# Where GpSimd issues the v gathers: behind the u gathers of two ticks later, instead of one

## The chip, the cores and the metric

The kernel runs on one core of a Trainium2 chip, in float32. The metric is device time in microseconds (us) of one execution, median of the runs shown.

## The reference

Two small networks run one after the other on 256 tokens of width 1024. The first is two layers of attention and MLP. The second is two layers of attention (a sparse one, "nsa", then one with forget gates, "fox"), each followed by a PEER feed-forward. This feed-forward is what the change touches: every token chooses 128 experts (8 heads x 16) out of 16384 by ranking scores, and each expert is one row of a table u and one of a table v.

```python
def one_chunk(args):
    xc, ec, gc = args                  # 128 tokens, their 128 experts, their gates
    h = jax.nn.gelu(jnp.einsum('ted,td->te', u[ec], xc))
    return jnp.einsum('te,ted->td', gc.astype(h.dtype) * h, v[ec])
```

## The kernel before

The first network, and the projections of the second's first attention, come first and take about 900 us of the span. Then follow four windows: two layers times two tiles of 128 tokens. A window is 128 expert slots, and a slot is one expert for each of the 128 tokens: a gather of 128 rows of 4 KB from u and one from v, by an indirect DMA that GpSimd issues. Four slots (SLICE) are a tick, so that a window has 32 ticks (TICKS) and the whole has 128, numbered here from 0 to 127.

In each tick every engine does its part of the four slots:

- GpSimd issues the gathers (`gather`, line 2290 for u and v alike). The buffers are rings of 8 slots, two ticks (RING), one for u (`urow`) and one for v (`vrow`). A gather into a ring waits until the slot of 8 before was used: for u the semaphore `u_used`, which VectorE raises at each dot, for v the semaphore `v_used`, which TensorE raises at each slot. A u gather also waits for `routed`, the choice of its experts.
- VectorE makes the dots with the token (`expert_dots`, line 1945; 'CUSTOM_DVE_ANT_0' in the trace, with the reading of the accumulator behind it).
- ScalarE makes the gelu and the gates and writes a diagonal matrix for each slot (`expert_gates`, lines 1389, 1394 and 1400).
- TensorE multiplies this diagonal with the v rows and adds up in two banks (`expert_slice`, line 925). A slot is 4 matmul records, the slice of a tick 16.

Beside this part each of TensorE, ScalarE and VectorE runs the rest of the second network in pieces between ticks: behind the slice, gates or dots of tick k comes what the plans (`STAGES`, `nsa_plan`, `fox_plan`, `LATE_ROUTE`) put at tick k. In the plans of attention VectorE's pieces stand one tick behind TensorE's (`added_late`). Examples are the masked scores (`soften`, line 1996, from TensorE's line 1014 or 1122), the weighted values (TensorE's line 1000, VectorE's reciprocals in lines 2011 and 2179), the transposes of line 991, the projections of line 945 with weight panels that SyncE loads, and the ranking of the next window's experts (lines 1861 to 1926). At the end of each window VectorE folds the sum into the residual (`fold`, line 1954); it waits for all of the window's slices, and TensorE's next slice waits for it. Every engine's instructions stand in program order on its queue.

Of the kernel before, what the change touches and what calls it, by code (L numbers as in the profile page):

```python
# [67 lines left out]
TICKS = SLOTS // SLICE  # L68
WINDOWS = [(layer, t) for layer in range(2) for t in range(TILES)]
# [91 lines left out]
    return base + WEIGHTS[name[0]] + int(name[1])  # L161


LATE_RANKS = [24, 25, 26, 27, 35, 36, 37, 38]
CHOSEN = [[(0, 1), (1, 3), (3, P_HEADS)]] + [[(0, P_HEADS // 2), (P_HEADS // 2, P_HEADS)]] * 3
CHOICES = {"route00": [-1, 1, 7], "route01": [28, 40], "route10": [28, 40], "route11": [28, 40]}
# [2 lines left out]
def ranked_at(stage, begin, head):  # L169
    if stage == "route00":  # L170
        return [-1, -1, 0, 2, 3, 4, 5, 6][head]
    return begin + LATE_RANKS[head]

# [9 lines left out]
def piece_of(window, slot):  # L183
    return pieces_before(window) + sum(first * TOPK <= slot for first, _ in CHOSEN[window])
# [102 lines left out]
def over(base, dims):  # L287

    return bass.AP(base.tensor, base.offset, [list(base.ap[0])] + [list(d) for d in dims])


def build(nc, x, panels, gains, consts, line_consts, rel_bias, lam, subln, small, fbias, keys, u0, v0, u1, v1, out,
# [3 lines left out]
    with ExitStack() as ctx:  # L296
# [241 lines left out]
        def apart(eng, *waits):  # L538


            for s, value in waits:
                eng.wait_ge(s, value)
            eng.sem_inc(waits_passed, 1)
# [42 lines left out]
        def filled(eng, key):  # L586

            eng.wait_ge(bank_filled, NUMBER[key] + 1)
# [8 lines left out]
        @block.sync  # L597
        def _(sp):
            sp.dma_start(h[:, :, :], x.rearrange("(t p) d -> p t d", p=P)).then_inc(first_loaded, 16)

            sp.wait_ge(first_loaded, 16 * 5)
            def load(n, half, slot):
                at = slice(half * PANEL // 2, (half + 1) * PANEL // 2)
                sp.dma_start(ring[:, slot, at], panels[n, :, at]).then_inc(landed[slot][half], 16)

            for s in range(2):
                if s == 1:
                    sp.wait_ge(landed[0][1], 16)
                for half in range(2):
                    load(s, half, s)  # L610
            pairs = N_PANELS // 2
            with sp.Fori(1, pairs) as i:
                for s in range(2):
                    for half in range(2):

                        sp.wait_ge(panel_used, i * 4 + (2 * s - 3 + half))
                        load(i * 2 + s, half, s)
            for n in range(2 * pairs, N_PANELS):
                for half in range(2):
                    sp.wait_ge(panel_used, 2 * n - 3 + half)  # L620
                    load(n, half, n % 2)
            for i, key in enumerate(USES):
                n = N_PANELS + i
                if i < 2:
                    sp.wait_ge(panel_used, 2 * (n - 1))
                else:
                    filled(sp, LAST_USE.get(USES[i - 2], USES[i - 2]))
                sp.dma_start(ring[:, n % 2, :], panels[panel_source(key)]).then_inc(landed[n % 2][0], 16)
            for t in range(TILES):
                sp.wait_ge(final_ready, t + 1)  # L630
                sp.dma_start(out[t * P:(t + 1) * P, :], xn[:, t, :]).then_inc(out_landed, 16)
            sp.wait_ge(out_landed, 16 * TILES)
# [582 lines left out]
        def _(act):  # L1215
# [248 lines left out]
            def soft_exps(stage, i):  # L1464
                key = stage, in_batch("S", 0, i)[-1]
                t, _, depth = block_of(key)
                keys_of = (t + 1) * P
                if i >= 2:
                    emptied(act, (stage, f"O{i - 2}"))
                act.wait_ge(peak_ready, softened(key))  # L1470
                for j in range(BATCH):
                    a = soft_of(key)[:, j * keys_of:(j + 1) * keys_of]
                    last = f(a, a, ACT.Exp, bias=peaks[i % 2][:, j:j + 1], accum_out=totals[i % 2][:, j:j + 1])
                last.then_inc(soft_ready, 1)
# [791 lines left out]
        @block.gpsimd  # L2266
        def _(pool):
            phase = Phases(pool)
            g = nc.gpsimd

            def stage_pairs(call):

                base, kind = PAIRS * call, KIND[call]
                with pool.Fori(0, PAIRS // 2) as i:
                    for u in range(2):
                        p = i * 2 + (base + u)

                        apart(pool, (s_done, p + (AHEAD - 1)))
                        g.tensor_copy(stage[u][:, :, 0, :], pj[:, :, bass.ds(i * (2 * P) + u * P, P)])  # L2279
                        last = g.tensor_copy(stage[u][:, :, 1, :], pj[:, :, bass.ds(i * (2 * P) + (D + u * P), P)])  # L2280
                        last.then_inc(staged, 1)

            def gather(rows, tables, there, tick):

                layer, t = WINDOWS[tick // TICKS]
                for n in range(tick * SLICE, (tick + 1) * SLICE):
                    s, slot = n % RING, n % SLOTS
                    if n >= RING:
                        pool.wait_ge(u_used if rows is urow else v_used, n - RING + 1)
                    g.indirect_dma_start(out=rows[s], out_offset=None, in_=tables[layer],  # L2290
                                         in_offset=bass.IndirectOffsetOnAxis(ap=experts[:, t, slot:slot + 1], axis=0))\
                        .then_inc(there[s], 16)

            for (step, arg), meets in zip(SCHEDULE, MEETS):
                if step == "attend":
                    stage_pairs(arg)
                elif step == "dense" and arg == "in0":

                    for slot in range(2):
                        pool.wait_ge(landed[slot][1], 16)  # L2300

                    pool.wait_ge(lines_ready, 1)
                    pool.dma_start(line_dram, lines).then_inc(lines_out, 16)
                    pool.wait_ge(lines_out, 16)
                    pool.dma_start(lines_dram.rearrange("p h l -> p (h l)"),
                                   bass.AP(line_dram.tensor, 0, [[0, P], [1, HEADS * LINE]])).then_inc(lines_out, 16)

                    pool.wait_ge(lines_out, 32)
                    later = bass.AP(lines_dram.tensor, P - 1, [[HEADS * LINE - 1, P], [LINE, HEADS], [1, SEQ]])
                    early = bass.AP(lines_dram.tensor, 2 * P - 1, [[HEADS * LINE - 1, P], [LINE, HEADS], [1, P]])  # L2310
                    pool.dma_start(bias[:, :, P:S_COLS], later).then_inc(lines_in, 16)
                    pool.dma_start(bias[:, :, 0:P], early).then_inc(lines_in, 16)
                    pool.dma_start(smallw[:, :], small).then_inc(loaded, 16)
                    for dst, src, n in ((subln_row, subln, 2 * HD), (fb_row, fbias, HEADS)):
                        pool.dma_start(dst[:, :], bass.AP(src.tensor, 0, [[0, P], [1, n]])).then_inc(loaded, 16)
                    pool.wait_ge(lines_in, 32)
                    pool.wait_ge(loaded, 16 * 3)
                if meets:
                    phase()
            for n in range(8):  # L2320
                piece, t = (0, 1, 2, 4)[n // 2], n % 2
                pool.wait_ge(roped, {0: 5 + t, 1: 6, 2: 7 + t, 3: 9 + t}[n // 2])
                if n == 7:
                    filled(pool, ("middle", "T3"))
                g.tensor_copy(twin[n].rearrange("p g (a b) -> p g a b", a=2),  # L2325
                              over(pj[:, t, KV_AT + piece * GROUPS * HD:], [[HD, GROUPS], [0, 2], [1, HD]]))\
                    .then_inc(twinned, 1)
            pool.wait_ge(proj_read, 2 * AHEAD + 2 * sum(WIDTH.values()))
            g.tensor_copy(kept_v, over(pj[:, 1, KV_AT + 3 * GROUPS * HD:], [[2 * GROUPS * HD, 2], [1, GROUPS * HD]]))\
                .then_inc(v_kept, 1)  # L2330
            for tick in range(-1, len(WINDOWS) * TICKS):

                after = tick + 1
                if after < len(WINDOWS) * TICKS:
                    pool.wait_ge(routed, piece_of(after // TICKS, after % TICKS * SLICE))
                    gather(urow, (u0, u1), u_landed, after)
                if tick >= 0:
                    gather(vrow, (v0, v1), v_landed, tick)
# [71 lines left out]
```

## Time and profile before

| | |
|---|---|
| median of 3 runs | 2504.35 us (2501.98 to 2504.45) |
| the profiled execution | 2505.09 us, span 2502.9 us |
| TensorE / VectorE / ScalarE / GpSimd busy | 85% / 57% / 35% / 40% |
| DMA, mean over the span | 302 GB/s |
| mean granted TensorE clock | 0.936 |

A row of the page or of a list of groups gives a source line, the engine (PE is TensorE, PEld its weight load, DVE VectorE, ACT ScalarE, POOL GpSimd), what is written and read, a count, then the busy time and the mean of one, and behind the last bar the idle time of the engine just ahead of these instructions with what ended it. Z is the large region in which `urow`, `vrow` and `diag` lie. A row of a timeline begins with the start in us from the span's start and the duration. A row of a stretch gives the engines in the order PE, PEld, DVE, ACT, POOL.

### The profile page before, as it was taken

How to read it: one execution, taken by the hardware profiler on the slowest of the kernel's cores; microseconds unless marked ns; L12 is line 12 of the kernel's file. 1: busy time of each engine (PE TensorE's matmuls, PEld its weight loads, DVE VectorE, ACT ScalarE, POOL GpSimd, SP SyncE). 2: the span in 40 equal slices, each digit the busy share in tenths (PEclk: the TensorE clock that was granted, in tenths of full speed). 3: DMA queues.
4: the chain of work that ended last, by engine and by line, in shares of the span. 5: the costliest groups of instructions: out<-in, count | busy, mean ns of one | idle time of the engine just before them, and what ended most of it. 6: DMA issues, size and time to landing. Idle time of an engine off the chain costs nothing.

```text
span 2502.9 us, 24203 instructions
## 1 busy us (share of the span) xinstructions
PE 2139.3 (85%) x7260; PEld 1252.2 (50%) x7260; DVE 1416.0 (57%) x3004; ACT 881.8 (35%) x2125; POOL 1000.2 (40%) x1076
## 2 busy tenths in 40 slices
PE   7889999799999876789987898897899898667676
PEld 5668878678877542354433343343445343223232
DVE  3474463554465458665485744476745457584443
ACT  3445444644534322463232243222234223221121
POOL 0100000000000046556656556656656656667664
PEclk9899999899999798899999998998999999888888
DMA  8325545055545279789999999999999999999997
GB/s 312 141 75 180 199 168 194 25 177 193 176 143 210 101 317 364 288 320 386 413 412 407 401 409 357 414 412 409 386 415 359 394 412 386 366 339 377 359 380 283
DMA packets 172681, 754.69 MB, mean 302 GB/s; under 512 B 19184, under 2 KB 19344, under 8 KB 152736
## 3 DMA queue, kind: packets, MB, share of 16 engines
q0 software_dynamic: 148640, 544.05, 56.2%
q1 hardware_dynamic: 21584, 197.14, 21.2%
q10 hardware_dynamic: 2352, 12.24, 1.3%
q8 instruction: 49, 0.80, 0.1%
q14 instruction: 56, 0.46, 0.0%
HBM read 752.28 MB, written 4.22 MB: 302 GB/s over the span
## 4 chain that ended last, share of the span: by engine, by line
PE 58%; DVE 10%; issue 9%; DMA 8%; POOL 8%; ACT 3%; another core or an unknown queue 2%; DVEq 1%; ACTq 0%; POOLq 0%; SPq 0%
PE ps L925 19%; PE ps L945 9%; POOL Z L2290 8%; PE ps L670 7%; PE ps L672 7%; PE ps L671 7%; DMA Z<-v,experts 6%; DVE Z L1945 3%; DMA ring<-panels 1%; PE ps L1000 1%; PE ps L1065 1%; DVE ring_lo L1767 1%; DMA Z<-u,experts 1%; PE ps L991 1%
## 5 line engine op out<-in xcount | busy, mean ns | idle before, releaser
L925 PE MATMUL ps<-Z 128*128 128x512 f32 x2048 | 991.0, 640 | 240.8 <-DMA Z<-v,experts 123.2
L925 PEld LDWEIGHTS ps<-Z 128*128 128x128 f32 x2048 | 410.9, 206 | 782.8 <-issue 608.5
L1945 DVE CUSTOM_DVE_ANT_0 Z<-Z,ps 128x1024 f32<-128x1024 f32 x512 | 605.7, 1219 | 270.3 <-DMA Z<-u,experts 209.2
L2290 POOL DMA_INDIRECT Z<-u,experts x512 | 487.2, 951 | 378.0 <-issue 156.8
L2290 POOL DMA_INDIRECT Z<-v,experts x512 | 489.2, 955 | 350.4 <-PE ps L925 162.6
L1767 DVE TENSOR_TENSOR ring_lo<-ring,ring_hi 128x1024 fp32r<-128x1024 f32 x212 | 247.7, 1221 | 191.6 <-ACT ring_hi L1231 191.4
L945 PE MATMUL ps<-ring,o 128*128 128x512 f32 x560 | 252.3, 605 | 10.5 <-issue 9.8
L670 PE MATMUL ps<-ring_hi,xT_lo 128*128 128x512 f32 x592 | 235.6, 398 | 12.7 <-DVE xT_lo L1815 7.5
L671 PE MATMUL ps<-ring_lo,xT 128*128 128x512 f32 x592 | 231.3, 391 | 0.0
L672 PE MATMUL ps<-ring_hi,xT 128*128 128x512 f32 x592 | 231.2, 391 | 0.0
L1231 ACT CAST ring_hi<-ring 128x1024 fp32r<-128x1024 f32 x212 | 209.0, 1051 | 40.0 <-DMA ring<-panels 37.5
L1400 ACT ACTIVATE Z<-cst,wslot 128x128 f32<-128x128 f32 x512 | 165.9, 392 | 95.9 <-remote 47.9
L1389 ACT ACTIVATE hdot<-hdot 128x4 f32<-128x4 f32 x128 | 26.5, 207 | 456.8 <-issue 235.8
L945 PEld LDWEIGHTS ps<-ring,o 128*128 128x128 f32 x560 | 107.0, 194 | 142.0 <-issue 141.0
L2279 POOL COPY Z<-pj 128x256 f32 x16 | 6.5, 406 | 410.4 <-ACTq L535 361.0
L670 PEld LDWEIGHTS ps<-ring_hi,xT_lo 128*128 128x128 f32 x592 | 111.6, 189 | 43.7 <-DVE ring_lo L1767 8.7
L2325 POOL COPY ksc<-pj 128x512 f32<-128x512 f32 x5 | 3.5, 713 | 303.8 <-DVE pj L1855 297.8
L672 PEld LDWEIGHTS ps<-ring_hi,xT 128*128 128x128 f32 x592 | 111.6, 188 | 23.7
L671 PEld LDWEIGHTS ps<-ring_lo,xT 128*128 128x128 f32 x592 | 111.7, 189 | 22.5 <-issue 0.5
L1394 ACT ACTIVATE wslot<-hdot,gate_w 128x1 f32<-128x1 f32 x512 | 109.4, 285 | 9.3 <-issue 0.7
L670 PE MATMUL ps<-ring_hi,hT 128*128 128x512 f32 x256 | 100.5, 392 | 1.4 <-DVE hT L1775 1.2
L672 PE MATMUL ps<-ring_hi,hT 128*128 128x512 f32 x256 | 99.7, 389 | 0.0
(271 smaller groups left out, 1968.4 us busy)
## 6 DMA issues: line engine op xcount, KB each, us to landing
ring<-panels SPq DMA_DIRECT2D x106, 1024.0 KB, 5.0
ring<-panels SPq DMA_DIRECT2D x40, 2048.0 KB
Z<-u,experts POOLq DMA_INDIRECT x512
Z<-v,experts POOLq DMA_INDIRECT x512
gain<-gains ACTq DMA_DIRECT2D x4, 1024.0 KB, 4.8
pj<-keys ACTq DMA_DIRECT2D x4, 1024.0 KB
bias_lines<-bias_line POOLq DMA_DIRECT2D x1, 3072.0 KB, 14.9
gain<-gains ACTq DMA_DIRECT2D x5, 512.0 KB, 3.7
```

The costliest lines, as they stand in the source:

```text
L670: mm(out, b, c, start=start, stop=False)
L671: mm(out, a, d, start=False, stop=False)
L672: return mm(out, a, c, start=False, stop=stop)
L925: last = mm(ps[:, c, :], diag[s], vrow[s][:, c * NC:(c + 1) * NC], start=slot == 0, stop=slot == SLOTS - 1)
L945: last = mm(to, tokT[:, k, :], w[:, k * NC:(k + 1) * NC], start=k == 0, stop=k == KT - 1)
L1231: copy(ring_hi[:, slot, c * CH:(c + 1) * CH], ring[:, slot, c * CH:(c + 1) * CH]).then_inc(hi_ready, 1)
L1389: f(cols, cols, ACT.Gelu_apprx_tanh)
L1394: f(own[:, s:s + 1], cols[:, s:s + 1], ACT.Copy, scale=gate_w[:, t, slot + s:slot + s + 1])
L1400: f(diag[n % RING], ident, ACT.Copy, scale=own[:, s:s + 1]).then_inc(diag_ready, 1)
L1767: v.tensor_tensor(ring_lo[:, slot, at], ring[:, slot, at], ring_hi[:, slot, at].bitcast(F32), ALU.subtract).then_inc(lo_ready, 1)
L1945: v.tensor_tensor_reduce(out=row, in0=row, in1=dotted, scale=1.0, scalar=0.0, op0=ALU.mult, op1=ALU.add, accum_out=hdot[:, t, slot:slot + 1])\
L2290: g.indirect_dma_start(out=rows[s], out_offset=None, in_=tables[layer], in_offset=bass.IndirectOffsetOnAxis(ap=experts[:, t, slot:slot + 1 ...
```

## The change

The loop in which GpSimd issues the gathers starts two ticks ahead instead of one. In its turn for a tick it issues the u gathers of two ticks later, and then the v gathers of the tick itself. Nothing else changes: the same 1024 gathers with the same waits on the same rings.

```diff
+V_BEHIND = 2
...
-            for tick in range(-1, len(WINDOWS) * TICKS):
-
-                after = tick + 1
+            for tick in range(-V_BEHIND, len(WINDOWS) * TICKS):
+
+                after = tick + V_BEHIND
                 if after < len(WINDOWS) * TICKS:
                     pool.wait_ge(routed, piece_of(after // TICKS, after % TICKS * SLICE))
                     gather(urow, (u0, u1), u_landed, after)
                 if tick >= 0:
                     gather(vrow, (v0, v1), v_landed, tick)
```

On GpSimd's queue, where the expert phase begins, stand before (with the semaphores that a row waits for; the first waits of a ring's first two ticks are absent):

```order
L2290 DMA Z<-u,experts 128x1024 [waits routed]
L2290 DMA Z<-u,experts 128x1024 x3
L2290 DMA Z<-u,experts 128x1024 [waits routed]
L2290 DMA Z<-u,experts 128x1024 x3
L2290 DMA Z<-v,experts 128x1024 x4
L2290 DMA Z<-u,experts 128x1024 [waits u_used,routed]
L2290 DMA Z<-u,experts 128x1024 [waits u_used] x3
L2290 DMA Z<-v,experts 128x1024 x4
```

The same place on GpSimd's queue in the changed kernel, whose lines have numbers higher by one:

```order
L2291 DMA Z<-u,experts 128x1024 [waits routed]
L2291 DMA Z<-u,experts 128x1024 x3
L2291 DMA Z<-u,experts 128x1024 [waits routed]
L2291 DMA Z<-u,experts 128x1024 x3
L2291 DMA Z<-u,experts 128x1024 [waits u_used,routed]
L2291 DMA Z<-u,experts 128x1024 [waits u_used] x3
L2291 DMA Z<-v,experts 128x1024 x4
L2291 DMA Z<-u,experts 128x1024 [waits u_used,routed]
L2291 DMA Z<-u,experts 128x1024 [waits u_used] x3
L2291 DMA Z<-v,experts 128x1024 x4
```

The four v gathers of tick 0 moved behind the four u gathers of tick 2, which wait for the dots of tick 0. At the end of GpSimd's queue stand before:

```order
L2290 DMA Z<-u,experts 128x1024 x4
L2290 DMA Z<-v,experts 128x1024 x4
L2290 DMA Z<-u,experts 128x1024 x4
L2290 DMA Z<-v,experts 128x1024 x8
```

And at the end of the same queue in the changed kernel:

```order
L2291 DMA Z<-u,experts 128x1024 x4
L2291 DMA Z<-v,experts 128x1024 x4
L2291 DMA Z<-u,experts 128x1024 x4
L2291 DMA Z<-v,experts 128x1024 x12
```

Behind the last four u gathers now stand the v gathers of three ticks instead of two.

## Rows read from the trace of the kernel before

**Rows 1.** The page: the costliest groups of the expert phase.

```profile
L925 PE MATMUL ps<-Z 128*128 128x512 f32 x2048 | 991.0, 640 | 240.8 <-DMA Z<-v,experts 123.2
...
L1945 DVE CUSTOM_DVE_ANT_0 Z<-Z,ps 128x1024 f32<-128x1024 f32 x512 | 605.7, 1219 | 270.3 <-DMA Z<-u,experts 209.2
...
L2290 POOL DMA_INDIRECT Z<-v,experts x512 | 489.2, 955 | 350.4 <-PE ps L925 162.6
```

**Rows 2.** Stretches: busy us (and count) by engine, granted clock, DMA share, GB/s.

```profile
1023.00:1163.00 140.00, 120.96 (x426) 66.92 (x427) 83.40 (x174) 72.89 (x205) 81.77 (x87) 0.88 0.87 319
1163.00:1303.00 140.00, 121.68 (x313) 55.91 (x312) 84.48 (x219) 36.23 (x111) 86.31 (x89) 0.96 1.02 413
...
1469.00:1567.00 98.00, 85.07 (x264) 41.87 (x263) 49.54 (x94) 41.34 (x128) 60.65 (x65) 0.93 0.97 374
...
1870.00:1945.00 75.00, 71.07 (x263) 40.18 (x262) 45.99 (x81) 35.49 (x101) 43.49 (x47) 0.95 0.97 366
1945.00:2130.00 185.00, 162.15 (x401) 73.03 (x399) 107.99 (x261) 51.26 (x165) 113.62 (x120) 0.95 1.01 398
...
2257.00:2503.00 246.00, 176.17 (x341) 71.42 (x340) 103.04 (x170) 49.17 (x183) 150.44 (x160) 0.88 0.91 350
```

**Rows 3.** Timeline of GpSimd: u gathers of tick 15, first v gather of tick 14.

```profile
1093.07 0.94 POOL L2290 DMA_INDIRECT Z<-u,experts  x1 [2.81 <-DVE hdot L1945]
...
1096.80 0.94 POOL L2290 DMA_INDIRECT Z<-u,experts  x1 [0.30 <-issue]
1098.05 0.94 POOL L2290 DMA_INDIRECT Z<-v,experts  x1 [0.30 <-issue]
```

**Rows 4.** Timeline of VectorE: the end of tick 13's dots, and a wait behind it.

```profile
1095.63 0.08 DVE L1945 DVE_READ_ACCUMULATOR2_ANT hdot<- 128x1 f32 x1
...
1104.48 0.18 DVE L2011 RECIPROCAL shares<-totals 128x4 f32<-128x4 f32 x1 [4.97 <-remote]
```

**Rows 5.** Timeline of ScalarE: the diagonals of tick 13.

```profile
1096.95 1.28 ACT L1400 ACTIVATE Z<-cst,wslot 128x128 f32<-128x128 f32 x4
```

**Rows 6.** Timeline of TensorE: the slices of ticks 13 and 14.

```profile
1099.21 7.03 PE L925 MATMUL ps<-Z 128*128 128x512 f32 x16
...
1113.63 8.41 PE L925 MATMUL ps<-Z 128*128 128x512 f32 x16
```

**Rows 7.** Groups of VectorE from 1023 to 1163 us.

```profile
L1996 DVE SCALAR_TENSOR_TENSOR scratch<-ps,cst 128x512 f32<-128x512 f32 x7 | 4.8, 687 | 12.2 <-remote 10.6 <-PE ps L1014 0.9 <-PE ps L991 0.7
...
L2011 DVE RECIPROCAL shares<-totals 128x4 f32<-128x4 f32 x8 | 1.4, 174 | 23.7 <-remote 23.7
```

**Rows 8.** Tail: timelines of GpSimd and TensorE at tick 120, chain at tick 125.

```profile
2405.91 0.94 POOL L2290 DMA_INDIRECT Z<-v,experts  x1 [2.54 <-PE ps L925]
...
2410.86 10.11 PE L925 MATMUL ps<-Z 128*128 128x512 f32 x16 [5.54 <-DMA Z<-v,experts]
...
2462.81 6.50 DMA Z<-v,experts
2469.36 8.27 PE ps L925 x16
```

**Rows 9.** Timelines of VectorE and TensorE: ticks 14, 44 and 78.

```profile
1110.31 0.08 DVE L1945 DVE_READ_ACCUMULATOR2_ANT hdot<- 128x1 f32 x1
...
1485.34 0.08 DVE L1945 DVE_READ_ACCUMULATOR2_ANT hdot<- 128x1 f32 x1
...
1488.43 5.42 PE L925 MATMUL ps<-Z 128*128 128x512 f32 x12 [0.88 <-issue]
...
1917.50 0.08 DVE L1945 DVE_READ_ACCUMULATOR2_ANT hdot<- 128x1 f32 x1
...
1919.36 7.11 PE L925 MATMUL ps<-Z 128*128 128x512 f32 x16
```

**Rows 10.** GpSimd's v gathers from 2257 to 2480 us, and the end.

```profile
L2290 POOL DMA_INDIRECT Z<-v,experts x80 | 75.2, 940 | 52.1 <-issue 23.8 <-remote 16.5 <-PE ps L925 11.5
...
2488.74 5.49 PE L925 MATMUL ps<-Z 128*128 128x512 f32 x12 [0.24 <-DMA Z<-v,experts]
```

## Prediction

> **What bounds the kernel now.** A tick is four expert slots: GpSimd gathers four u rows and four v rows per token, VectorE makes four dots, ScalarE four gates, TensorE four weighted sums (a "slice"). I read the page first: TensorE's slice line and VectorE's dot line are the costliest groups, and both, with GpSimd's v gathers, wait a lot [rows 1]. 128 ticks at four rows of 128 x 4 KB for u and for v are what sets the pace, so next I cut the expert phase into stretches [rows 2]. They are of two sorts. In the first sort (1163 to 1303, and most of 1303 to 2130) the DMA share is 1.01 to 1.02 and 398 to 413 GB/s: the transfers are the bound. In the second (1023 to 1163, 1469 to 1567, 1870 to 1945; I call them the locked stretches) the share is 0.87 to 0.97, with 319 to 374 GB/s: something makes the queue run short. The tail from 2257 runs at 0.91 and 350 GB/s.
>
> Then the timelines of one locked place. GpSimd issues a gather every 1.245 us; its first u row waits for VectorE's dot of two ticks before, in the row's own words "DVE hdot" [rows 3]. VectorE's dots of tick 13 end at 1095.63 + 0.08 = 1095.71; then it waits for what TensorE computed behind the slice of tick 12, 4.97 us ahead of the reciprocal (put down to a remote releaser, since the ScalarE and TensorE work that it needs was long recorded) [rows 4]. ScalarE has the four gate diagonals from 1096.95 on [rows 5]. TensorE starts the slice of tick 13 at 1099.21 without any idle time, as it does tick 14's at 1113.63 [rows 6]. So here nobody waits for v: the v rows were issued one tick before and are simply there, and the loop is VectorE's step, dots, gates, slice, TensorE's step behind the slice, VectorE's step one or two ticks on. Over the first locked stretch VectorE stands idle 12.2 us ahead of one of the two groups of masked scores and 23.7 us ahead of the reciprocals, all for TensorE's or ScalarE's part [rows 7]. VectorE's lateness is GpSimd's too, through the u buffers.
>
> **The change.** Instructions, bytes and the alternation u, v, u, v stay. Before, v of tick k is issued behind u of tick k+1; now behind u of k+2. Both rings hold two ticks, so u of k+2 must wait for the dots of tick k. What is new is therefore a dependence: **v of tick k can't be issued before the dots of tick k are done and four more u gathers are issued.** Seen from the queue, v of k takes the place that v of k+1 had. In the prologue v of tick 0 falls behind four u gathers which wait for VectorE; at the end twelve v gathers follow the last u gather, instead of eight. Behind the waiting u gather on GpSimd's queue there is now the v that TensorE needs next, not the one after it.
>
> *When v arrives.* In the rows of tick 13, the last dot ends 1095.71 and the gather behind the last u one starts 1098.05, 2.3 us later [rows 3, 4]. That place now belongs to v of tick 13. From the start of an issue to the start of a slice that waited for just this gather: 2405.91 to 2410.86, 4.95 us [rows 8]; the chain at the end has a longer one, 2462.81 to 2469.36, 6.5 us, of which the row says 6.50 DMA [rows 8]. I take 5.3, nearer the former, since the locked stretches' queues are not full. So v is usable 2.3 + 5.3 = 7.6 us after the last dot. TensorE wants it at 1099.21; it gets it at 1103.3: 4.1 us late. The same at tick 14 (dots end 1110.39, usable 1118.0, slice 1113.63): 4.4. Tick 44 (1485.42, 1493.0, 1488.43): 4.6. Tick 78 (1917.58, 1925.2, 1919.36): 5.8 [rows 6, 9]. Mean 4.7; slices that start later behind other TensorE work lose less, so 4.5 for a slice. From below a slice loses nothing, where TensorE is far behind the dots; from above it loses a tick of transfers, about 10 us (8 x 1.245), where the queue is full.
>
> The Trainium skill (DMA: Bandwidth & Descriptors, "Anatomy of one DMA — SWDGE (gpsimd) path") fits a gather by about 2.0 us and bytes over 436e3, which for 512 KB is an estimate of 3.2 us instead of 5.3. By it a slice would lose 2.4 instead of 4.5 us, and the sum below would be some 27 us smaller. The trace's own waits are longer, so I keep them.
>
> *Locked stretches.* Ticks 8 to 17, 43 to 50 and 75 to 80: 24 slices. A late slice makes TensorE's step behind it late, this makes VectorE late, and so dots, u and v of two ticks on. Two such chains run interleaved, so each slice's loss counts half in the period: 24 x 4.5 / 2 = **54 us**. Entering each stretch the first loss counts whole, half of 4.5 more, three times: **7 us**.
>
> *Transfer-bound stretches.* There the order of bytes is as before and the rate can't fall; TensorE trails the dots by some 2.5 ticks instead of 1.5. This costs nothing until VectorE needs something of TensorE: the fold at each window's end, the score copies for the ranking, the projections of the next mixer. Then up to one tick, 10 us, comes out, less the slack of TensorE's panels. Before the second and third locked stretch I put 4 us each: **8 us** (0 to 20); at the rest nothing, covered by the transfers still queued; 3 us at each of six places, 18, if that cover is gone.
>
> *Ticks 0 to 7.* VectorE is bound by its own ranking, TensorE's slices come late and nobody waits: 0. What covers them is VectorE's work, and the first locked tick then pays (counted above).
>
> *Tail.* GpSimd's issue is on the chain; it waits for v buffers 52.1 us ahead of 80 gathers, 80 x 0.3 of this the usual gap, so 28 us of stalls [rows 10]. These waits are for the slice of two ticks before, and their distance doesn't change. At the end the last 12 matmuls run from 2488.74 for 5.49 us, 1.8 us a row of v, behind a wait for v [rows 10]. Now twelve rows follow the last u gather: four more at TensorE's 1.78 us a row, 7.03 us / 4 for a full-speed slice as in [rows 6]: **7 us**.
>
> Sum: 54 + 7 + 8 + 7 = 76 us. The profiled execution took 2505.09 us (span 2502.9), 0.7 over the median of 2504.35, so 2505.1 + 76 = 2581, and 2580 against the runs shown.
>
> **Rivals.**
> 1. *Hidden after all, only the end is paid.* v is late by the trace's arithmetic, but TensorE may have slack at most of these slices (the 4.97 us wait has a remote releaser, so part of VectorE's idle time may not follow TensorE's slice). Then the end's 7 us and a few at the entries: 2505 + 7 + 5 = 2517. Against it: TensorE's slices in [rows 6] have no idle time ahead.
> 2. *Faster.* The place is GpSimd's wait for v buffers in the tail and the panel-heavy ticks. A v gather that waits now holds back u of three ticks on instead of two; VectorE never starves behind it, dots and gates come earlier, TensorE runs the moment v lands and frees its buffers sooner. Its price is at most the 28 us of the tail [rows 10]: 2505 - 28 + 7 = 2484. It decides if slices in the tail start on gates, not on v; but [rows 8] have the slice waiting for the v gather, which no u order speeds up.
> 3. *Much slower.* TensorE's new wait of 4 to 5 us is one ahead of which its clock falls: 16 matmuls took 10.11 us behind 5.54 us of idle, against 7.03 without [rows 6, 8]; 24 slices at 1.7 to 3 us more, and the 18 us of the uncovered places: 2581 + 40 + 18 = 2640. (The Trainium skill, TensorE: Matmul & The Clock Gate, "What's actually happening", has the clock fall to half after idle time; the trace agrees in those two rows.)
>
> **How the numbers follow.** Forecast (2535 to 2615) 0.72; hidden 0.12; faster 0.06; much slower 0.10. A difference of 0.2%, 5 us, is about what a measurement of this kernel can tell. The low end takes half of a slice's loss, 2.25 us (24 x 2.25 / 2 = 27, 3 at the entries, 7 at the end: 2542), and reaches on towards the hidden case: 2525. The high end takes 5.8 a slice (70), 9 for its first losses, 20 for the entries and 7 at the end, 2611, and some of the clock: 2625. The likeliest one's own range is 2535 to 2615. Faster 0.06, same 0.04 (the hidden case with a cheap end), slower 0.90.
>
> **What would show it.** TensorE's slices of ticks 8 to 17 with idle time of 3 to 5 us ahead, released by the DMA of v; the three locked stretches longer (140 to about 165 us, 98 to 122, 75 to 95) with a lower DMA share; the transfer-bound stretches as long as now at a share of 1.02; VectorE's waits for TensorE longer in total; u's part of VectorE's 270.3 us of waiting [rows 1] smaller. I am wrong if slices in the locked stretches still start without idle time, or if the length comes from the transfer-bound stretches, or if the tail's ticks get shorter.

## The result, and the profile after

| | before | after |
|---|---|---|
| median of the runs | 2503.16 us (2491.15 to 2504.45, 4 runs) | 2576.14 us (2574.27 to 2581.68, 4 runs) |
| ratio | | 1.0306 [1.0280, 1.0331] |
| span of the profiled execution | 2502.9 us | 2572.1 us |
| mean granted TensorE clock | 0.936 | 0.922 |

The change costs 73 us; 76 were forecast. The page of the changed kernel, whose line numbers are higher by one, has these groups in place of [rows 1]; of GpSimd's two the one of the u gathers is shown, for its wait:

```profile
L926 PE MATMUL ps<-Z 128*128 128x512 f32 x2048 | 1027.1, 659 | 307.1 <-DMA Z<-v,experts 252.7
...
L1946 DVE CUSTOM_DVE_ANT_0 Z<-Z,ps 128x1024 f32<-128x1024 f32 x512 | 600.7, 1218 | 201.9 <-DMA Z<-u,experts 144.3
L2291 POOL DMA_INDIRECT Z<-u,experts x512 | 483.8, 945 | 551.2 <-DVE hdot L1946 279.9
```

TensorE's wait for v has doubled (123.2 to 252.7 us), VectorE's wait for u has shrunk (209.2 to 144.3), and GpSimd's u gathers now wait for the dots (279.9 of 551.2 us): v stands behind the dots, and the slice behind v. The slices are also slower in themselves, 1027.1 us against 991.0.

The stretches that answer to those of [rows 2] are cut here at the starts of slices: 8 to 18, then what follows, 43 to 51, 75 to 81, and 107 to 127 (columns as there):

```profile
1034.60:1183.00 148.40, 119.55 (x417) 63.55 (x418) 71.18 (x152) 61.36 (x174) 81.11 (x87) 0.87 0.84 311
1183.00:1320.00 137.00, 123.78 (x313) 56.46 (x311) 84.80 (x222) 36.78 (x111) 76.86 (x81) 0.95 1.02 411
...
1510.20:1619.40 109.20, 87.68 (x246) 42.02 (x244) 54.74 (x105) 38.43 (x120) 64.49 (x68) 0.91 0.91 343
1932.30:2016.90 84.60, 71.64 (x243) 38.60 (x242) 40.68 (x74) 33.78 (x101) 50.41 (x54) 0.90 0.85 313
2339.10:2556.40 217.30, 163.12 (x320) 66.24 (x321) 88.47 (x144) 49.47 (x176) 140.66 (x151) 0.90 0.96 368
```

The locked stretches' DMA share is 0.84, 0.91 and 0.85 (0.87 to 0.97 in [rows 2]); the transfer-bound one runs at 1.02 and 411 GB/s as before. One locked tick, number 11, first in VectorE's timeline (start, duration, what; in brackets the idle time ahead):

```profile
1063.32 1.21 DVE L1946 CUSTOM_DVE_ANT_0 Z<-Z,ps 128x1024 f32<-128x1024 f32 x1
...
1067.88 0.08 DVE L1946 DVE_READ_ACCUMULATOR2_ANT hdot<- 128x1 f32 x1
1073.20 0.69 DVE L1997 SCALAR_TENSOR_TENSOR scratch<-ps,cst 128x512 f32<-128x512 f32 x1 [5.24 <-PE ps L1015]
```

Then in GpSimd's:

```profile
1065.31 0.94 POOL L2291 DMA_INDIRECT Z<-u,experts  x1 [3.48 <-DVE hdot L1946]
...
1070.27 0.94 POOL L2291 DMA_INDIRECT Z<-v,experts  x1 [0.31 <-issue]
```

In ScalarE's:

```profile
1069.19 1.28 ACT L1401 ACTIVATE Z<-cst,wslot 128x128 f32<-128x128 f32 x4
```

And in TensorE's, with the slices of ticks 10, 11 and 12:

```profile
1063.51 8.52 PE L926 MATMUL ps<-Z 128*128 128x512 f32 x16 [4.97 <-DMA Z<-v,experts]
1071.96 1.14 PE L1015 MATMUL ps<-gain,pj 64*128 64x256 f32 x8
...
1076.79 7.13 PE L926 MATMUL ps<-Z 128*128 128x512 f32 x16 [0.88 <-DMA Z<-v,experts]
...
1091.14 10.06 PE L926 MATMUL ps<-Z 128*128 128x512 f32 x16 [3.34 <-DMA Z<-v,experts]
```

The dots of tick 11 end at 1067.96. The first v gather of the tick starts 2.3 us later, at 1070.27, as forecast, and its slice 6.5 us behind that, at 1076.79, where 5.3 were taken. ScalarE had the diagonals at 1070.5, so it is not they that the slice waited for. The slice ahead of it, tick 10's, waited 4.97 us for v; so TensorE's scores behind it (line 1015) came late, and VectorE stood 5.24 us for them: the round trip that the prediction describes. Of the three slices shown the two behind a wait of 3 to 5 us take 8.52 and 10.06 us, the one behind 0.88 takes 7.13. The granted clock (third from the end of a row: 1.00 is 2.4 GHz, and lower values mix it with 1.2 GHz) was lower during these two:

```profile
1063.51:1072.03 8.52, 8.52 (x18) 3.58 (x18) 4.45 (x8) 6.57 (x20) 5.20 (x6) 0.83 0.87 312
1076.79:1083.92 7.13, 7.13 (x18) 3.02 (x18) 5.70 (x14) 6.02 (x18) 3.01 (x4) 1.00 0.69 247
1091.14:1101.20 10.06, 10.06 (x18) 4.12 (x18) 5.76 (x14) 6.64 (x20) 3.75 (x4) 0.71 0.61 219
```

Where the 69.2 us of the two spans came from, by how much later a slice starts than before: 4.3 at tick 8, 20.8 at 18, 32.9 at 43, 45.6 at 51, 37.9 at 68, 52.3 at 81, 72.2 at 93, 75.6 at 107, 69.8 at 127, 69.2 at the end. So the locked stretches and what leads into the first and the third gave 4.3 + 16.5 + 12.7 + 14.4 = 48 us. The others gave +12.1 (ticks 18 to 43), -7.7 (51 to 68), +19.9 (81 to 93), +3.4 (93 to 107) and -6.4 (the tail and end), 21 us together.

### The profile page after: what moved, and what is told of

The parts are those of the page before. It is cut to its first block, busy times and chain, and to the rows that moved or that the text cites. A ratio compares the mean times of both kernels' runs of the same rounds, so it can differ in the third digit from the quotient of the medians.

```text
span 2572.1 us, 24203 instructions
## 1 busy us (share of the span) xinstructions
PE 2169.9 (84%) x7260; PEld 1259.7 (49%) x7260; DVE 1410.7 (55%) x3004; ACT 884.4 (34%) x2125; POOL 996.1 (39%) x1076
## 4 chain that ended last, share of the span: by engine, by line
PE 46%; DVE 16%; DMA 11%; POOL 9%; issue 8%; another core or an unknown queue 4%; ACT 3%; DVEq 1%; ACTq 0%; POOLq 0%; SPq 0%
PE ps L926 13%; POOL Z L2291 9%; DMA Z<-v,experts 9%; DVE Z L1946 7%; PE ps L671 7%; PE ps L673 7%; PE ps L672 7%; PE ps L946 5%; DMA ring<-panels 1%; PE ps L1066 1%; DVE ring_lo L1768 1%; DMA Z<-u,experts 1%; PE ps L1001 1%; PE ps L661 1%
## 5 line engine op out<-in xcount | busy, mean ns | idle before, releaser
L926 PE MATMUL ps<-Z 128*128 128x512 f32 x2048 | 1027.1, 659 | 307.1 <-DMA Z<-v,experts 252.7
L926 PEld LDWEIGHTS ps<-Z 128*128 128x128 f32 x2048 | 421.4, 211 | 876.0 <-issue 532.9
L1946 DVE CUSTOM_DVE_ANT_0 Z<-Z,ps 128x1024 f32<-128x1024 f32 x512 | 600.7, 1218 | 201.9 <-DMA Z<-u,experts 144.3
L2291 POOL DMA_INDIRECT Z<-u,experts x512 | 483.8, 945 | 551.2 <-DVE hdot L1946 279.9
L1401 ACT ACTIVATE Z<-cst,wslot 128x128 f32<-128x128 f32 x512 | 172.9, 392 | 338.2 <-PE ps L926 142.5
L1390 ACT ACTIVATE hdot<-hdot 128x4 f32<-128x4 f32 x128 | 26.1, 204 | 287.8 <-DVE hdot L1946 183.3
```

The source lines that it names most:

```text
L926: last = mm(ps[:, c, :], diag[s], vrow[s][:, c * NC:(c + 1) * NC], start=slot == 0, stop=slot == SLOTS - 1)
L1390: f(cols, cols, ACT.Gelu_apprx_tanh)
L1401: f(diag[n % RING], ident, ACT.Copy, scale=own[:, s:s + 1]).then_inc(diag_ready, 1)
L1946: v.tensor_tensor_reduce(out=row, in0=row, in1=dotted, scale=1.0, scalar=0.0, op0=ALU.mult, op1=ALU.add, accum_out=hdot[:, t, slot:slot + 1])\
```

## The experiments

My theory: v of tick k can't be issued before the dots of tick k; where TensorE and VectorE run in lockstep (ticks 8 to 17, 43 to 50, 75 to 80), each slice loses some 4.5 us, half of it in the period. The rivals: the loss is in the other stretches or at the end, or it is the clock, or it isn't the wait for the dots that does it.

The runs were made in sets of two speeds, in which the same kernel before took about 2418 and 2500 us. They are called the quicker and the slower chip here, though that it is the chip which differs is not shown: chip number 1 stands on record beside a set of either speed. Each run is therefore compared with runs of the kernel before on its own chip, and sizes in us of one chip aren't taken over to the other. Runs 1 to 4 and 8 to 11 are from chips with 2418 us, 5 to 7 from one with 2500, as is the result above.

**1. Only the locked stretches** (label e1_locked_only). v stands behind two ticks in these 24 ticks alone. The lines behind the dots take the place of the whole loop of before.

```diff
+LOCKED = [*range(8, 18), *range(43, 51), *range(75, 81)]
...
+            v_next = 0
+            for tick in range(len(WINDOWS) * TICKS + 2):
+                if tick < len(WINDOWS) * TICKS:
+                    pool.wait_ge(routed, piece_of(tick // TICKS, tick % TICKS * SLICE))
+                    gather(urow, (u0, u1), u_landed, tick)
+                while v_next < len(WINDOWS) * TICKS and v_next + (2 if v_next in LOCKED else 1) <= tick:
+                    gather(vrow, (v0, v1), v_landed, v_next)
+                    v_next += 1
```

> v stands behind the u rows of two ticks later in the 24 ticks 8 to 17, 43 to 50 and 75 to 80 alone, and behind one elsewhere. My theory (a late v makes TensorE and then VectorE late in the locked stretches): slower than the kernel before by 45 to 55 us, about 2552 us, with TensorE's slices there 13 us behind the start of the dots instead of 6.4. Rival (the loss lies in the transfer-bound stretches and at the end): slower by 10 us at most.

Measured: 2469.54 us against 2417.84, ratio 1.0217 [1.0200, 1.0234], +52 us. For the first locked stretch (slice 8 to 18) the kernel before, profiled on such a chip (run 11) has this row of the stretch, and these groups of TensorE and VectorE in it:

```profile
1025.00:1130.90 105.90, 105.85 (x417) 58.92 (x418) 76.46 (x162) 67.63 (x190) 76.49 (x83) 0.99 1.02 400
```

```profile
L925 PE MATMUL ps<-Z 128*128 128x512 f32 x161 | 72.6, 603 | 2.2 <-ACT Z L1400 2.2
...
L1996 DVE SCALAR_TENSOR_TENSOR scratch<-ps,cst 128x512 f32<-128x512 f32 x6 | 4.1, 686 | 8.4 <-PE ps L1014 8.4
```

And e1_locked_only has, with GpSimd's u gathers among the groups:

```profile
1032.10:1162.90 130.80, 114.47 (x417) 62.02 (x418) 70.63 (x152) 60.87 (x173) 78.08 (x84) 0.92 0.89 333
```

```profile
L926 PE MATMUL ps<-Z 128*128 128x512 f32 x161 | 80.5, 657 | 25.6 <-DMA Z<-v,experts 25.6
...
L2291 POOL DMA_INDIRECT Z<-u,experts x40 | 37.5, 937 | 39.6 <-DVE hdot L1946 29.7 <-issue 9.9
...
L1997 DVE SCALAR_TENSOR_TENSOR scratch<-ps,cst 128x512 f32<-128x512 f32 x6 | 4.1, 686 | 26.9 <-PE ps L1015 26.9
```

TensorE waits 25.6 us for v where it waited for none, its slices take 8 us more at a lower granted clock, and VectorE waits 27 instead of 8 us for its scores: 105.9 us become 130.8. Against that profile this kernel's slices are late by 32.0 us at tick 18, 28.3 at 32, 37.5 at 51, 54.8 at 81 and 49.1 at the end. So the three stretches, with the lateness at their entries, cost 32 + 9 + 17 = 58 us, and 9 of it is given back outside them. Within the 24 ticks it is 44 us (24.9, 5.6 and 13.5).

**2. Everywhere else** (e2_rest_only): the same loop with `v_next not in LOCKED`.

> The complement: behind two ticks everywhere except in ticks 8 to 17, 43 to 50 and 75 to 80. By the sum of my prediction: 7 us at the end, 8 at the entries, about 2518 us. By the profile after, which has some 20 us lost between ticks 82 and 93: slower by 20 to 30 us, about 2528 us. Rival (everything is lost here): slower by 60 us or more.

Measured: 2437.44 us against 2417.84, ratio 1.0088 [1.0071, 1.0105], +20 us. The two parts add up to 51.7 + 19.6 = 71.3 us or 3.05%. The whole change cost 3.06% and 3.21%, 73 and 75 us, but on the slower chip; on the quicker one it was not run. Against run 11's profile its slices are at most some 3 us late up to tick 81, then 7.7 at 85, 13.9 at 93, 19.6 at 100, and 16.2 at the end. So it isn't spread over all transfer-bound ticks. It is lost in ticks 81 to 100, the end of the third window with the ranking for the fourth, its fold and the step after.

**3. Only ticks 81 to 93** (e6_ticks_81_93): the loop of run 1 with `LOCKED = range(81, 94)`.

> v behind u of two ticks later in ticks 81 to 93 alone, a transfer-bound stretch in which VectorE waits once for the scores of the next window's ranking and once for the last projections of the mixer. The profile after has some 20 us lost there, my prediction nothing. If those 20 us belong to this place: slower than the kernel before by 10 to 20 us. If they are an echo of what was lost earlier: slower by 5 us at most.

Measured: 2422.48 us against 2417.30, ratio 1.0021 [1.0011, 1.0030], +5 us: by the total this is the rival's size, not the 10 to 20 us of my theory. The trace shows the place's price and a gain behind it: from tick 81 to 93 it lost 12.5 us (4.9 by tick 83, 1.3 more by 86, 6.4 by 93), and from 93 to 100, where v moves up again by one u block, it got 5.4 back (68.4 against 73.8 us), where run 2 lost 5.7 more. So the place has a price of its own of some 12 us, with nothing lost ahead of it; the way back to the old order repays about half.

**4. Only the tail and the end** (e11_tail): `LOCKED = range(107, 128)`.

> v behind u of two ticks later from tick 107 on alone, so that twelve v gathers follow the last u gather. Nothing of attention runs there. By my prediction's term for the end: slower than the kernel before by 5 to 8 us. Rival (in the tail the waits for v buffers swallow it): within 2 us.

Measured: 2419.45 us, ratio 1.0006 [0.9997, 1.0015], +2 us, which no measurement here tells from nothing. TensorE's timeline at the end of the kernel before (run 11):

```profile
2384.37 7.13 PE L925 MATMUL ps<-Z 128*128 128x512 f32 x16 [3.11 <-DMA Z<-v,experts]
2394.61 14.00 PE L925 MATMUL ps<-Z 128*128 128x512 f32 x32 [3.11 <-DMA Z<-v,experts]
```

and of e11_tail:

```profile
2377.62 8.83 PE L926 MATMUL ps<-Z 128*128 128x512 f32 x16 [3.09 <-DMA Z<-v,experts]
2387.86 20.87 PE L926 MATMUL ps<-Z 128*128 128x512 f32 x48 [1.41 <-DMA Z<-v,experts]
```

The end is at 2394.61 + 14.00 = 2408.61 before and 2387.86 + 20.87 = 2408.73 now. Three slices in a row instead of two do stand behind the last u rows, but TensorE had 3.11 us of idle time ahead of each slice, and the third fits where these were: it starts 6.75 us sooner. In run 11 the slice behind 3.11 us of idle time took 7.13 us: not every wait of this length is followed by a slow slice.

**5. The changed kernel once more** (after_again), as the base for runs 6 and 7.

> The changed kernel again, as the measure for the runs beside it: slower than the kernel before by 65 to 80 us.

Measured: 2573.79 us against 2499.11, ratio 1.0321 [1.0277, 1.0365], +75 us.

**6. u and v row by row** (e4_alternating). As in the changed kernel v of tick k goes with u of k+2, but one u and one v in turn, so that the first v row of a tick is issued three gathers earlier. The waits on rings stay. (`gather` gets the rows to issue as a further argument; the loop starts two ticks ahead.)

```diff
-                    gather(urow, (u0, u1), u_landed, after)
-                if tick >= 0:
-                    gather(vrow, (v0, v1), v_landed, tick)
+                for one in range(SLICE):
+                    if after < len(WINDOWS) * TICKS:
+                        gather(urow, (u0, u1), u_landed, after, [one])
+                    if tick >= 0:
+                        gather(vrow, (v0, v1), v_landed, tick, [one])
```

> v again behind u of two ticks later, but row by row: one u gather, one v gather. The first v gather then waits for one dot alone instead of four, and is usable some 9 us behind the start of the dots instead of 13.3; the last of the four ends its row at 18.4 instead of 20.4. By my theory (a slice ends late by 4.9 instead of 6.9 us): slower than the kernel before by 45 to 60 us. If the number of bytes queued ahead of v matters and not the dots: the same as the changed kernel.

Measured: 2572.92 us, ratio 1.0305 [1.0260, 1.0349], the same as the changed kernel: a miss. TensorE's timeline in a locked tick:

```profile
1074.90 1.98 PE L925 MATMUL ps<-Z 128*128 128x512 f32 x4
1078.14 1.98 PE L925 MATMUL ps<-Z 128*128 128x512 f32 x4 [1.25 <-DMA Z<-v,experts]
1081.16 1.98 PE L925 MATMUL ps<-Z 128*128 128x512 f32 x4 [1.04 <-DMA Z<-v,experts]
1083.67 1.98 PE L925 MATMUL ps<-Z 128*128 128x512 f32 x4 [0.52 <-DMA Z<-v,experts]
1085.58 1.14 PE L1014 MATMUL ps<-gain,pj 64*128 64x256 f32 x8
```

The slice starts earlier, but it now waits for each of its rows and lasts 10.7 us, so that the scores behind it come no sooner. It is the last v row of a tick that counts for VectorE, and this row stands where it stood. The run also says something of the clock: its mean granted clock was 0.948, where run 5 had 0.925, and in its first locked stretch 0.93 against 0.87 of the changed kernel, at the same length (148.5 and 148.4 us). So a higher granted clock alone didn't bring the time back.

**7. VectorE's and ScalarE's attention pieces a tick later** (e7_later_steps, e8_control): in `added_late` the plans' tick + 2 in place of tick + 1, in the changed kernel and in the kernel before. This widens the slack between TensorE's piece and VectorE's, through which a late slice reaches the dots.

```diff
-    return sorted([(tick + 1 + (name[0] in "fu"), name) for tick, names in plan for name in names], key=lambda m: m[0])
+    return sorted([(tick + 2 + (name[0] in "fu"), name) for tick, names in plan for name in names], key=lambda m: m[0])
```

> The changed kernel, with VectorE's pieces of attention two ticks behind TensorE's in the plan instead of one. The gathers stay as changed. If the loss comes by way of VectorE's waits for TensorE in the locked stretches, this takes a good part of it away: 15 to 35 us faster than the changed kernel. Rival (TensorE's own wait for v is the whole loss, whatever VectorE does): within 5 us of the changed kernel, or slower since TensorE now waits for the softmax.

> The same shift of VectorE's pieces in the kernel before, as the control. There VectorE waits some 45 us for TensorE in the first locked stretch, but TensorE itself never waits for v: within 10 us of the kernel before, on either side.

Measured: with the change 2533.89 us, ratio 1.0157 [1.0116, 1.0198] to the kernel before, 40 less than run 5. Without the change 2473.05 us, ratio 0.9905 [0.9873, 0.9938], 26 less than the kernel before on the same chip: a miss for the control, and **faster than both kernels**. The first locked stretch in the kernel before and in e8_control:

```profile
1030.30:1162.20 131.90, 118.19 (x417) 64.96 (x418) 76.29 (x162) 67.93 (x190) 77.51 (x84) 0.89 0.90 331
```

```profile
1032.50:1146.70 114.20, 108.50 (x416) 59.34 (x417) 72.75 (x157) 67.66 (x190) 73.91 (x80) 0.98 0.98 367
```

So the lockstep bounds the kernel before itself on this chip, and slack between the two engines' pieces is worth 17.7 us in this stretch and 17.4 in the third (82.7 to 65.3 us). Of the 40 us that the same edit saves in the changed kernel, some 14 are more than it saves without the change. So of the 15 to 35 us that were expected by way of VectorE's waits the control leaves 14, not far above the scatter (runs of one kernel differ by up to 16 us here). With this slack the change still costs 61 us (2533.89 - 2473.05), 22.5 of them in the first locked stretch, whose row and TensorE's slices in e7_later_steps are:

```profile
1031.90:1168.60 136.70, 118.31 (x417) 65.93 (x418) 76.98 (x162) 67.78 (x192) 81.17 (x87) 0.88 0.91 338
```

```profile
L926 PE MATMUL ps<-Z 128*128 128x512 f32 x161 | 76.3, 629 | 2.0 <-DMA Z<-v,experts 1.9
```

TensorE waits only 2.0 us for v in this stretch (37.3 in the changed kernel), and the stretch is still longer than e8_control's. What costs there is not shown; of the 28.1 us that VectorE waits for the masked scores 26.1 are put down to a remote releaser. On the chips with 2418 us the kernel before needs only 105.9 and 64.8 us there already, and this edit wasn't run on them.

**8. Only the wait** (e3_wait_only): the order of before, and ahead of the v gathers of a tick the wait for its dots.

```diff
                     gather(urow, (u0, u1), u_landed, after)
                 if tick >= 0:
+                    pool.wait_ge(u_used, (tick + 1) * SLICE)
                     gather(vrow, (v0, v1), v_landed, tick)
```

> The order of before, but the v gathers of tick k also wait for the dots of tick k. If the wait for the dots is the cause, v is usable 0.8 + 5.9 = 6.7 us behind the last dot instead of 8.7, 5 us late instead of 7, so five sevenths of the locked loss and nothing at the end: slower by 30 to 40 us, about 2538 us. If the place of v behind four more u gathers is the cause: slower by 10 us at most.

Measured: 2451.69 us, ratio 1.0145 [1.0128, 1.0162], +34 us, nearly half of the 71 us that runs 1 and 2 give together on this chip, and within the 30 to 40 us expected. Its first locked stretch, and groups of TensorE and VectorE in it:

```profile
1025.70:1143.00 117.30, 110.89 (x416) 59.13 (x417) 74.03 (x158) 62.70 (x176) 79.05 (x85) 0.97 0.98 375
```

```profile
L925 PE MATMUL ps<-Z 128*128 128x512 f32 x160 | 76.1, 626 | 12.3 <-DMA Z<-v,experts 12.2
...
L1945 DVE CUSTOM_DVE_ANT_0 Z<-Z,ps 128x1024 f32<-128x1024 f32 x43 | 50.3, 1214 | 10.4 <-DMA Z<-u,experts 10.2
```

TensorE waits 12.2 us for v, half of run 1's 25.6; the other half goes with the four u gathers ahead of v, the only other difference in this stretch. Here u pays for it: VectorE waits 10.2 us for u, and none in run 1 (3.6 in run 11).

**9. v behind the u rows of its own tick** (e5_behind_own): the loop issues u and then v of the same tick, one tick earlier than before.

> One step the other way: v of tick k directly behind u of tick k. By my theory the locked stretches gain nothing, since TensorE did not wait for v there; the end gains the 7 us that the change lost, and the transfer-bound stretches up to 10 more by a shorter lag of TensorE: 2486 to 2498 us. Rival (u now stands behind v gathers that wait for TensorE, and VectorE starves): slower than before by 5 us or more.

Measured: 2420.32 us, ratio 1.0013 [1.0004, 1.0023], +2.5 us: a miss, and the rival's 5 us or more didn't come either. On the page of e5_behind_own most of TensorE's wait is no longer for v:

```profile
L925 PE MATMUL ps<-Z 128*128 128x512 f32 x2048 | 980.4, 636 | 203.2 <-ACT Z L1400 177.1
L1945 DVE CUSTOM_DVE_ANT_0 Z<-Z,ps 128x1024 f32<-128x1024 f32 x512 | 613.3, 1219 | 447.4 <-DMA Z<-u,experts 433.4
```

and on that of the kernel before on such a chip (run 11):

```profile
L925 PE MATMUL ps<-Z 128*128 128x512 f32 x2048 | 967.2, 628 | 215.9 <-DMA Z<-v,experts 187.3
L1945 DVE CUSTOM_DVE_ANT_0 Z<-Z,ps 128x1024 f32<-128x1024 f32 x512 | 609.0, 1218 | 324.8 <-DMA Z<-u,experts 311.9
```

An earlier v turns most of TensorE's wait for v (187.3 us) into a wait for the gates (177.1), and VectorE's wait for u grows from 311.9 to 433.4 us, at the same time within 3 us: here the order only decides who waits. Later costs, earlier gains nothing.

**10. A tick later still** (e10_steps_3): `added_late` with tick + 3 in the kernel before.

> The kernel before with VectorE's pieces of attention three ticks behind TensorE's instead of one; two ticks were 26 us faster. If VectorE's waits for TensorE are gone at two, three gives nothing more or costs some (TensorE then waits for the softmax): 2 to 15 us slower than two ticks were, so 10 to 25 us faster than the kernel before. If waits remain: up to 10 us faster than two ticks.

Measured: 2456.12 us against 2417.30, ratio 1.0157 [1.0142, 1.0173], +39 us: a miss in sign. Groups of TensorE and VectorE in the third locked stretch, which became 84.7 us long instead of 64.8:

```profile
L1000 PE MATMUL ps<-pj,scratch 128*128 128x64 f32 x32 | 7.4, 424 | 6.8 <-ACT scratch L1408 6.8
...
L2179 DVE RECIPROCAL shares<-totals 128x4 f32<-128x4 f32 x4 | 0.7, 178 | 21.7 <-PE ps L1000 21.7
```

TensorE's weighted values need the probabilities that VectorE and ScalarE make from the scores. With VectorE's piece so late, TensorE waits for them (6.8 us, none before on this chip), and VectorE 21.7 us for the values. My reading is that the slack goes both ways round the loop, and more on one side is less on the other. The two-tick version wasn't tried on the quicker chip, nor this one on the slower.

**11. The kernel before** (before_again), for a profile on a chip like that of runs 1 to 4 and 8 to 10.

> The kernel before once more, for its profile on this chip: within 0.3% of the kernel before's other runs on this chip, with the locked stretch of ticks 8 to 18 some 20 us shorter than in the runs with v behind two.

Measured: 2419.34 us, span 2417.2, granted clock 0.952.

## Why the prediction was right, and where only its sum was

**The mechanism** held where it could be tested singly. v needs the dots of its own tick (run 8: the wait alone +34 us), the locked stretches carry most of it (run 1: +52 of the 71 us of runs 1 and 2), VectorE's wait for TensorE's scores grew (8.4 to 26.9 us in one group of run 1's first stretch), and u's part of VectorE's waiting shrank (209.2 to 144.3 us). Run 7 leaves a part of it open on the slower chip: with more slack TensorE hardly waits for v in the first stretch, and the change costs 61 us still.

**When v arrives.** The 2.3 us from the last dot to the issue was right. The 5.3 us from issue to slice were too few: 6.5 in the tick shown, and 8.5 to 8.9 us from last dot to slice in ticks 10 to 12, 14 and 15, where 7.6 were taken. The Trainium skill (DMA: Bandwidth & Descriptors, "Anatomy of one DMA — SWDGE (gpsimd) path") has a fit that gives 3.2 us for 512 KB as an estimate. The trace doesn't agree: it has 6.5 us in that tick, in a stretch whose DMA share is 0.84.

**Locked stretches** were put at 54 + 7 + 8 = 69 us. The result gave 48. Of these 31 lie within the 24 ticks (16.5, 12.7 and 1.9), for which 54 were forecast, and 17 at the entries, for which 15 were. So the term of 54 us is the one that was mis-sized. The stretches didn't lengthen to 165, 122 and 95 us as told: from slice to slice they went from 131.9 to 148.4, 96.5 to 109.2, and 82.7 to 84.6 with 12.5 more just ahead (ticks 68 to 75). Run 1, on the quicker chip, gave 44 within the 24 ticks and 14 at the entries.

One reason is the choice of the slices from which 4.5 us was taken. Those of ticks 13, 14, 44 and 78 start 1.8 to 3.5 us behind their last dot. In the same trace the slices of all 24 ticks start 1.8 to 22.2 us behind it, and five of them more than 7.6, so that a v at 7.6 us costs them nothing. The same working over all 24 gives a mean of 3.2 us and a term of 39; with v at 8.6 us, as measured, it is 4.0 and 49.

The rest, down to 31, is argued and not shown. The kernel before on the slower chip had waits in these stretches already (of VectorE, 12.2 and 23.7 us in [rows 7]), and part of the new wait seems to have taken their place. In the first stretch VectorE's waits ahead of the masked scores and the reciprocals grew from 45.0 to 56.2 us on the slower chip, where the stretch grew by 16.5, and from 20.9 to 45.6 in run 1 on the quicker, where it grew by 24.9. No run takes those waits away alone.

**Transfer-bound stretches** were put at 0, with 18 if the cover was gone. The cover was gone, at the place named for it: ranking and fold of ticks 81 to 100 (run 2: +20 us; the result: +20 in ticks 81 to 93). VectorE's group of the ranking's first step, between ticks 76 and 91, in the kernel before and in the changed one:

```profile
L1861 DVE MAX8 ranks<-ksc 128x8 f32<-128x128 f32 x8 | 1.9, 283 | 11.8 <-ACT ksc L1408 11.8
```

```profile
L1862 DVE MAX8 ranks<-ksc 128x8 f32<-128x128 f32 x8 | 1.9, 284 | 21.9 <-ACT ksc L1409 21.9
```

VectorE waits 10 us longer there for the scores, which stand behind TensorE's slices. This is the step that failed: the cover was called sufficient from the DMA share, and the tick that TensorE trails was not followed to the fold. The other half of the 20 us isn't assigned to a wait. At the first window's fold, ahead of the slice of tick 32, TensorE stood 11.81 us for VectorE in the changed kernel; the slices fell 8 us further behind between ticks 30 and 32. On the quicker chip run 2 shows no such loss (0.8 us late at tick 18, 1.8 at 32).

**The tail and end** were put at 7. Run 4 measured 2, and in the result the tail took 6 us less than before (217.3 us against 223.0 from slice 107 to 127), 5.6 of them in its last seven ticks. In run 4 the idle time ahead of each slice took the third one in. The working counted four more rows at TensorE's rate and didn't ask where TensorE had been waiting.

So the sum of 76 met 73 by luck, because two misses cancel: some 20 too many in the locked stretches, some 20 too few elsewhere.

**Its own signs.** The waits for v, the longer locked stretches with a lower DMA share, and the shorter waits for u all came. But two of the three signs that were to show it wrong came too, at least in part: 21 of the 69 us come from outside the locked stretches, and the tail got shorter. They count against the account of the places, not against that of the wait, which runs 1 and 8 test.

**The rivals.** Hidden (2517) and faster (2484) fell with the result; run 9 adds that an earlier v gains nothing either. Much slower (2640) fell as a sum, but both of its parts are in the result. The uncovered places are one. The clock is the other: TensorE's slices are busy 36 us longer (991.0 to 1027.1). The granted clock was 0.71 in the slice of 10.06 us behind 3.34 us of idle time and 1.00 in that of 7.13 behind 0.88. The Trainium skill (TensorE: Matmul & The Clock Gate, "What's actually happening") has the clock fall after idle time; those two rows agree, while run 11's slice of 7.13 us behind 3.11 us of idle time, at a granted clock of 1.00, shows that such a wait doesn't always bring it. How much of the 73 us is the slower clock, no run separates; run 6, with a higher clock and the same time, speaks against a large part.

## What to carry to other kernels

When a queue's order is changed, ask what the moved transfer now waits for through the instructions ahead of it, and whether that is the same round trip that its user is in: then each round pays, and the order costs time although no byte is added. When a loss per tick is taken from a few ticks, take it from all: the four looked at here gave 4.7 us, all 24 by the same working 3.2. The spare time between two engines' pieces is worth tuning for itself (one tick more gave 0.95% here on one chip, two more cost 1.6% on another), and a price for the end of a kernel has to be set against the idle time of the engine that ends it.

## What the runs showed of the hardware that was not expected

The same kernel ran at about 2418 and 2500 us, 3.4% apart, by the set of runs; what differs between the sets (called the two chips above) isn't known. It isn't a general slowness: the first slice starts at 929.4 us in run 11 and at 925.6 in the kernel before at 2503, so that all of the difference arises in the expert phase. On the slower one TensorE's signals seem to reach others late at times. One row each of the timelines of TensorE, GpSimd and ScalarE in the kernel before, near tick 112:

```profile
2298.24 17.38 PE L925 MATMUL ps<-Z 128*128 128x512 f32 x32 [5.47 <-DMA Z<-v,experts]
...
2317.74 0.94 POOL L2290 DMA_INDIRECT Z<-v,experts  x1 [2.75 <-remote]
...
2317.51 0.40 ACT L1400 ACTIVATE Z<-cst,wslot 128x128 f32<-128x128 f32 x1 [6.88 <-remote]
```

Both GpSimd and ScalarE waited there for row 443 to be used, whose matmuls, in the first half of these 32, are recorded as ended at 2308.34 (the ends of matmuls are modelled), and both went on 9.2 to 9.4 us later, at one time. In the whole trace 23 waits of GpSimd ahead of gathers, 62.3 us, are put down to such a remote releaser, and none in the traces of run 1 and run 11 on the quicker chip. From slice 107 to 127 the two take 223.0 and 202.5 us:

```profile
2263.60:2486.60 223.00, 166.61 (x321) 67.95 (x321) 93.43 (x152) 48.88 (x182) 145.35 (x155) 0.88 0.96 366
```

```profile
2199.10:2401.60 202.50, 148.61 (x321) 61.94 (x322) 93.38 (x152) 48.20 (x182) 140.52 (x150) 0.97 1.01 403
```

The tail is bound by its transfers on the quicker chip (403 GB/s), and loses part of that on the slower. What makes the signals late wasn't tried.
